# Gate pieces moved from the recurrence heads into prompt attention, and recurrence levels computed on half blocks

## The reference

```python
(q, k, v, iq, ik, iw, hq, hf, hi, hg, ga, gb) = jnp.split(h @ w_in, IN_OFFSETS, axis=-1)
...
merged = jax.nn.sigmoid(ga) * (attn @ w_proj_attn) + jax.nn.sigmoid(gb) * (o.reshape(B, T, WIDTH_B) @ w_proj_hgrn)
return merged @ w_out, k, v, ik, s_new
```

## Time and profile before

| | before |
|---|---|
| median of 3 runs (lowest to highest) | 1691.05 us (1688.89 to 1693.5) |
| time of the profiled execution | 1692.5 us |
| its span, first to last instruction | 1690.7 us |
| PE / DVE / ACT / POOL busy | 96% / 44% / 27% / 41% of the span |
| PE in the chain that ended last | 88% |
| mean granted TensorE clock | 0.983 |

### The profile page before, as it was taken

The page is one execution under the profiler, slowest core; times in us unless marked ns, Lnnn a source line. Parts: engine busy times, 40 slices in busy tenths (PEclk is TensorE's granted clock), DMA queues, the critical chain, the costliest instruction groups (busy, mean ns, idle before and its releaser), DMA issues.

```text
span 1690.7 us, 29123 instructions
## 1 busy us (share of the span) xinstructions
PE 1619.6 (96%) x12753; PEld 1498.2 (89%) x12753; DVE 735.9 (44%) x1138; ACT 452.3 (27%) x645; POOL 696.1 (41%) x580
## 2 busy tenths in 40 slices
PE   7999999999999999989889889988999999999998
PEld 6999999999976999988867655568999999999998
DVE  6422112224326689974587643345543321023221
ACT  4211112112354224422134333322232211112111
POOL 3443444546431345573542323334443343433432
PEclk9999999999999999997989899999999999999999
DMA  6322334333411232322252388995222322323222
GB/s 166 93 75 60 86 101 117 94 85 111 161 56 40 66 103 75 100 68 84 82 190 71 132 302 338 412 359 218 86 75 76 94 67 73 105 75 95 65 70 91
DMA packets 195230, 203.59 MB, mean 120 GB/s; under 512 B 6416, under 2 KB 181584, under 8 KB 186656
## 3 DMA queue, kind: packets, MB, share of 16 engines
q1 hardware_dynamic: 175344, 107.92, 22.3%
q0 software_dynamic: 12256, 77.93, 12.3%
q10 hardware_dynamic: 7504, 15.88, 2.5%
HBM read 187.21 MB, written 14.30 MB: 119 GB/s over the span
## 4 chain that ended last, share of the span: by engine, by line
PE 88%; DVE 7%; ACT 2%; issue 2%; DMA 1%; POOL 0%; SPq 0%; ACTq 0%; DVEq 0%
PE ps L1696 24%; PE ps L1697 24%; PE ps L1698 24%; PE ps L2167 4%; PE ps L2184 2%; PE ps L2242 1%; DVE att L1385 1%; DVE n_lo L1126 1%; DVE k_lev L1405 1%; PE ps L2075 1%; PE ps L2030 1%; PE ps L1709 1%; DVE prob_p L1467 1%; PE ps L2122 1%; DMA v_more<-in_cache_v,kv_row 1%
## 5 line engine op out<-in xcount | busy, mean ns | idle before, releaser
L528 POOL TENSOR_TENSOR w_lo<-raw,w_hi 128x512 fp32r<-128x512 f32 (+1 forms) x390 | 515.8, 1353 | 707.5 <-ACT w_hi L704 707.5
L1696 PE MATMUL ps<-n_lo,w_hi 128*128 128x288 f32 x1824 | 546.8, 300 | 1.0 <-ACT qT L818 1.0
L1697 PE MATMUL ps<-n_hi,w_lo 128*128 128x288 f32 x1824 | 540.1, 296 | 0.0
L1698 PE MATMUL ps<-n_hi,w_hi 128*128 128x288 f32 x1824 | 538.5, 295 | 0.0
L1696 PEld LDWEIGHTS ps<-n_lo,w_hi 128*128 128x128 f32 x1824 | 344.3, 189 | 11.2 <-issue 10.1
L1698 PEld LDWEIGHTS ps<-n_hi,w_hi 128*128 128x128 f32 x1824 | 345.5, 189 | 0.0
L1697 PEld LDWEIGHTS ps<-n_hi,w_lo 128*128 128x128 f32 x1824 | 344.7, 189 | 0.1
L704 ACT ACTIVATE w_hi<-raw 128x2048 fp32r<-128x2048 f32 (+2 forms) x108 | 188.2, 1742 | 273.3 <-PE ps L1698 271.1
L1697 PE MATMUL ps<-hid_hi,w_lo 128*128 128x288 f32 x704 | 208.4, 296 | 0.0
L1696 PE MATMUL ps<-hid_lo,w_hi 128*128 128x288 f32 x704 | 208.4, 296 | 0.0
L1698 PE MATMUL ps<-hid_hi,w_hi 128*128 128x288 f32 x704 | 208.1, 296 | 0.0
(11 more groups left out here) (305 smaller groups left out, 2246.6 us busy)
## 6 DMA issues: line engine op xcount, KB each, us to landing
raw<-in_ffn_w_gate SPq DMA_DIRECT2D x44, 512.0 KB, 4.0
raw<-in_ffn_w_up SPq DMA_DIRECT2D x44, 512.0 KB, 5.2
raw<-in_ffn_w_down SPq DMA_DIRECT2D x32, 704.0 KB, 4.6
raw<-in_w_in SPq DMA_DIRECT2D x22, 1024.0 KB, 5.3
gates<-scratch_g ACTq DMA_DIRECT2D x4, 1152.0 KB, 10.6
raw<-in_w_out SPq DMA_DIRECT2D x4, 1024.0 KB, 5.0
scratch_x<-xT ACTq DMA_DIRECT2D x1, 2304.0 KB, 12.1
scratch_g<-g_head SPq DMA_DIRECT2D x16, 144.0 KB, 1.8
```

The costliest lines, as they stand in the source:

```text
L528: ins = pool.tensor_tensor(w_lo[:, u % NRAW, part], raw[:, u % NRAW, part], w_hi[:, u % NW, part].bitcast(F32), ALU.subtract)
L1696: pe.matmul(dst, hi, x_lo, start=first, stop=False)
L1697: pe.matmul(dst, lo, x_hi, start=False, stop=False)
L1698: return pe.matmul(dst, hi, x_hi, start=False, stop=last)
```

## The change

1. `IN_HEADS` goes from 16 to 8: the pieces in the tails are gone. The heads keep the four of each pair's levels. Prompt attention has two pieces in each of steps 0 to 7 and one in each of steps 8 to 13. The second bank for pieces is bank 5, so in steps 0 to 7 both halves of a transpose go into bank 4 (`turn_banks`).
2. ACT copies a step's pieces out after the exponentials of the next step, not before. PE waits for a piece's bank through `gate_out`.
3. POOL's `low_part` inside the levels is gone; whole units are made low between them. Six units instead of four are scaled and stored by POOL in prompt attention, and one quarter instead of two is scaled at the projections.
4. Levels 1 to 7: the matmuls stream only the right halves, 64 columns a tile instead of 128, into 256 columns of a bank, and DVE's masked copy has 256 elements instead of 512. For the last two levels (b = 32 and 64) ACT copies the blocks without a mask (`block_out`).
5. `v_own` is made by DVE, between the levels and the state updates.
6. Five `EARLY` rounds instead of six. Four half rounds a step instead of three, so that the list ends in step 5; the exchange of lists is in step 7 and the work on the bias in steps 8 to 10.

```diff
-    return (3, 2, 0, 1)[n // 2]
+    return (n // 2 + 3) % 4
...
-        IN_HEADS = 16
-        UNITS_IN_HEADS = IN_HEADS // 4
-
+        IN_HEADS = 2 * HB
         STEPS = 2 * HA
-
-        def head_bank(i):
-
-            return i % 4 if i // 4 % 2 == 0 else (1, 6, 1, 0)[i % 4]
+        NARROW = HA
+
+        def pieces_of_step(m):
+
+            if m < NARROW:
+                return [IN_HEADS + 2 + 2 * m, IN_HEADS + 3 + 2 * m]
+            i = IN_HEADS + 2 + NARROW + m
+            return [i] if i < PIECES else []
+
+        def gate_bank(i):
+
+            if i < IN_HEADS:
+                return i % 4
+            if i == IN_HEADS:
+                return 6
+            return 5 if i % 2 == 0 and i < IN_HEADS + 2 + 2 * NARROW else 7
+
+        def score_banks(m):
+
+            return ps[:, 2 * (m % 2):2 * (m % 2) + 2, :]
+
+        def turn_banks(m):
+
+            return ps[:, 4, :].rearrange("p (e w) -> p e w", e=2) if m < NARROW else ps[:, 4:6, :]
...
+        def right_half(x, L):
+
+            return x.rearrange("p (n s b) -> p n s b", s=2, b=LEVELS[L])[:, :, 1, :]
+
+        ACT_LEVEL = 6
...
-                for n in range(UNITS_IN_HEADS, 8):
+                for n in range(2, 8):
...
-                for q in (2, 3):
-                    pool.wait_ge(S(f"quarter_in{q}"), X_IN[q] + 16)
-                    for n in range(2):
-                        for a in range(2):
-                            part = gates[:, GATES_AT[q] + n, a, :]
-                            ins = pool.tensor_tensor(part, part, rms[:, :], ALU.mult)
-                    ins.then_inc(S("gate_scaled"), 1)
+                pool.wait_ge(S("quarter_in3"), X_IN[3] + 16)
...
-                    if 3 <= L <= 6:
-                        low_part(L - 3)
...
-                lows(at_unit["gate", 2 * g + 2 if g == 0 else 4])
+                lows(at_unit["gate", g + 1])
                 state_store(2 * g)
                 state_store(2 * g + 1)
-            lows(at_unit["gate", 5])
+            lows(at_unit["gate", 3])
...
-            def own_values(h):
-
-                a, g = h % 2, h // 2
-                if g:
-                    act.wait_ge(S("head_read"), 2 * g)
-                else:
-                    act.wait_ge(S("prompt_biased"), 1)
-                for b in range(NB):
-                    ins = act.activation(v_own[:, a, b, :], stage[0:NS, g, 0, a * VD:(a + 1) * VD], ACT.Copy,
-                                         scale=cst[0:NS, C_OWN + NQ * b:C_OWN + NQ * b + 1])
-                ins.then_inc(S("v_own_done"), 1)
+            def block_out(g, a, L):
+
+                b = LEVELS[L]
+                act.wait_ge(S(f"level_done{a}"), 8 * g + L + 1)
+                act.wait_ge(S(f"level_out{a}"), 8 * g + L)
+                scores = ps[:, 4 + a, 0:256].rearrange("p (i n b) -> p i n b", i=4, b=b)
+                for n in range(P // (2 * b)):
+                    at = 2 * b * n
+                    ins = act.activation(att[at:at + b, a, :, at + b:at + 2 * b], scores[at:at + b, :, n, :], ACT.Copy)
+                ins.then_inc(S(f"level_out{a}"), 1)
 
             def heads(g):
-                act.wait_ge(S("stage_done"), NTOK + g + 1)
-                for a in range(2):
-                    own_values(2 * g + a)
-                for i in range(8 * g, 8 * g + 4):
+                for i in range(4 * g, 4 * g + 3):
                     gate_out(i)
+                for L in range(ACT_LEVEL, len(LEVELS)):
+                    for a in range(2):
+                        block_out(g, a, L)
+                gate_out(4 * g + 3)
...
-                    for i in range(8 * g + 4 + 2 * a, 8 * g + 6 + 2 * a):
-                        gate_out(i)
...
-                    if IN_HEADS + 1 + m < PIECES:
-                        if IN_HEADS + 1 + m == 28:
-                            act.wait_ge(S("pp_max"), m + 1)
-                        gate_out(IN_HEADS + 1 + m)
...
+                    for i in pieces_of_step(m - 1) if m else [IN_HEADS + 1]:
+                        gate_out(i)
                     if m:
                         turned(m - 1)
...
-            EARLY = 6
+            EARLY = 5
...
+                    b = LEVELS[L]
+                    n = P // (2 * b)
+                    if b < NQ:
+                        dve.copy_predicated(right_half(att_s[:, a, :], L), right_half(m[0:NS, 0:NS], L),
+                                            ps[0:NS, 6 + a, 0:NS // 2].rearrange("p (n b) -> p n b", b=b))
+                    dve.copy_predicated(mine.rearrange("p i (n s b) -> p i n s b", s=2, b=b)[:, :, :, 1, :],
+                                        right_half(m, L).unsqueeze(1).to_broadcast([P, 4, n, b]),
+                                        bank[:, 0:256].rearrange("p (i n b) -> p i n b", i=4, b=b)
+                                        ).then_inc(S(f"level_out{a}"), 1)
...
+                        if L - 1 < ACT_LEVEL:
+                            level_out(a, L - 1)
...
-                    level_out(a, 7)
+                for a in range(2):
+                    v0 = stage[0:NS, g, 0, a * VD:(a + 1) * VD]
+                    dve.tensor_tensor(v_own[:, a, :, :], v0.unsqueeze(1).to_broadcast([NS, NB, VD]),
+                                      cst[0:NS, C_OWN:C_OWN + NS:NQ].unsqueeze(2).to_broadcast([NS, NB, VD]),
+                                      ALU.mult).then_inc(S("v_own_done"), 1)
...
-                    for _ in range(3):
+                    for _ in range(4):
                         if taken[0] < 2 * ROUNDS:
                             take_half()
...
-                    if m == 7:
+                    if m == 5:
+                        assert taken[0] == 2 * ROUNDS
                         dve.engine_nop().then_inc(S("lists_done"), 1)
-                    if m == 9:
+                    if m == 8:
                         chosen_of_halves()
                         boundary()
+                    if m == 9:
+                        whole_rounds()
+                        last_round()
                     if m == 10:
-                        whole_rounds()
-                    if m == 11:
-                        last_round()
                         sample_biases()
...
-                if part[0] == 0 and not head:
-                    pe.wait_ge(S("gate_out"), i if i > IN_HEADS + 1 else i - 1)
-                bank = head_bank(i) if head else 6 if i == IN_HEADS else 7
+                if part[0] == 0 and i >= 4:
+                    one = i >= IN_HEADS + 2 + 2 * NARROW
+                    pe.wait_ge(S("gate_out"), i - 3 if i < IN_HEADS else i if one else i - 1)
+                bank = gate_bank(i)
...
+                            for t in range(1, NT):
+                                ins = pe.matmul(ps[:, 4 + a, P * (t - 1):P * t], key[:, h, cols(t)], query[:, h, cols(t)],
+                                                start=True, stop=True)
+                        else:
+                            if LEVELS[L] < NQ:
+                                pe.matmul(ps[0:NS, 6 + a, 0:NS // 2], k_lev[:, a, 0:NS], right_half(q_lev[:, a, 0:NS], L),
+                                          start=True, stop=True)
+                            for t in range(1, NT):
+                                ins = pe.matmul(ps[:, 4 + a, 64 * (t - 1):64 * t], k_lev[:, a, cols(t)],
+                                                right_half(q_lev[:, a, cols(t)], L), start=True, stop=True)
                         ins.then_inc(S(f"level_done{a}"), 1)
-                    gate_piece(8 * g + L // 2, (L % 2,))
+                    gate_piece(4 * g + L // 2, (L % 2,))
...
-                    if a:
-                        pe.wait_ge(S("o_out"), 2 * g + 1)
-                    else:
-                        pe.wait_ge(S("gate_out"), 8 * g + 4)
-                    tail = 8 * g + 4 + 2 * a
-                    gate_piece(tail, (0,))
-                    pe.wait_ge(S("k_rows_done"), 2 * g + 2)
+                    pe.wait_ge(S("k_rows_done"), h + 1)
+                    pe.wait_ge(S("gate_out"), 4 * g + 4)
...
-                            gate_piece(*((tail, (1,)), (tail + 1, (0,)), (tail + 1, (1,)))[i - 1])
...
+                    if m == NARROW:
+                        pe.wait_ge(S("gate_out"), IN_HEADS + 1 + 2 * NARROW)
...
+                dots(0)
                 pe.wait_ge(S("state_s_done"), HB)
-                dots(0)
                 gate_piece(IN_HEADS + 1, (0, 1))
...
-                    if IN_HEADS + 2 + m < PIECES:
-                        gate_piece(IN_HEADS + 2 + m, (0, 1))
+                    for i in pieces_of_step(m):
+                        gate_piece(i, (0, 1))
                     if m:
                         values(m - 1)
                     turn(m)
```

More of the change, by code:

```diff
@@ L510, in _ @@
                 load_unit(u)
[L511 removed]
+                if n in (0, 1):
                     store_piece(4 * n + 3)
@@ L529, in lows @@
                                                  w_hi[:, u % NW, part].bitcast(F32), ALU.subtract)
```

(10 more changed lines are left out.)

78 lines of the change are left out of this document (38 added, 40 removed).

## The result

The changed kernel takes 1701.4 us (median; 1700.26 to 1703.58) against 1691.05 for the kernel before: a ratio of 1.0063, 95% interval 1.0047 to 1.0079. Slower by 0.6%, outside the range, on the side to which the forecast gave 0.18. What follows splits up the 7.9.

A forecast was written before the change was run, and what follows sets the result against it. PE, busy 96% of the span, was taken to bound the kernel. Levels -6.2, tails -21.5 and prompt attention +22 sum to -5.7 us: from 1692.5, less 1.45 to the median, 1685.4, put at 1686; range 1675 to 1699.

The forecast's parts named there:

- Levels, -6.2: Levels of both head pairs: 3.1 us less a pair, 6.2 in all, from 3 to 9.
- (2): Levels: POOL's w_lo part of 1.48 us leaves four levels of each pair, which helps DVE too.
- (1): Levels: DVE's att copy shrinks to 128x256, about 0.27 us less, twice a level; ACT copies in the last two.
- (3): Levels: matmuls stream 64 columns instead of 128, at 0.24 us each instead of 0.27, saving 0.3 us a level.
- Tails, -21.5: Tails of both head pairs: eight half pieces fewer in each, 21.5 us less together, from 9 to 29.
- one tail of each kind: Tails: one at full clock, one with low clock after its first head; 14.5 + 7 = 21.5 us gained.
- rival (C): Tails: clock low from the first state update on; +7 to +10 us, 1698 with both tails; chance 0.22.
- Prompt attention, +22: Prompt attention with eight more pieces: 20.4 us more in steps 0 to 7, 1.7 in 8 to 13; 18 to 27.
- the wait for piece A: Prompt attention, steps 0 to 7: PE waits 0.7 us a step for ACT's later bank copy, 5.2 us in all.
- the half-clock prices: Tails at low clock: second head's updates 5.3 us for 2.5, sample matmuls 3.4 for 2.2, v_own matmuls 3.5 for 1.9.
- A's 0.16: Rival on the tails: both keep the full clock, gain 29 us instead of 21.5, so 1678; chance 0.16.
- The argument against (C): Tails: the clock outlived 1.95 us of near idleness ahead of 836.84, longer than the 1.5 us wait in question.

The follow-up runs named there:

- e5: The kernel of e2 with POOL's subtraction of the next gate unit held until both k transposes are done; ratio to the kernel before 0.9995.
- e1: The changed kernel with POOL's low part of a gate unit back in four quarters in levels 3 to 6; ratio to the kernel before 1.0007.
- e2: The changed kernel with v_own made by ACT at the start of the heads, as before the change; ratio to the kernel before 1.0015.
- e10: The changed kernel with v_own on ACT, POOL's unit after the k transposes and ACT's piece copies ahead of the exponentials; ratio to the kernel before 0.9921.
- e14: The kernel of e10 with v_own left on DVE, as in the changed kernel; ratio to the kernel before 0.9945.
- e8: The changed kernel with ACT's piece copies ahead of a step's exponentials in prompt attention, as before the change; ratio to the kernel before 1.0000.
- e15: The changed kernel with seven of the eight eight-column matmuls of each head left out; ratio to the kernel before 1.0025.
- e9: The changed kernel itself measured once more, nothing changed; ratio to the kernel before 1.0057.

## Why the prediction was wrong, step by step

- **Levels, -6.2: measured -5.2.** The period of 3.5 us came where it was said (from level 4 to level 7 of pair 0: 3.4, 3.5, 3.6). Level 2 of pair 0 took 6.6 us where pair 1's took 4.4, 1.7 us of it for the clock at half. The reason was in part wrong: of the three edits put together there, (2), POOL's quarters, carries 3.5 to 4.0 us, and (1) and (3) together 1.2 to 1.7, which the clock in pair 0 takes back. Term (3), 0.3 us a level, measured 0.2 in level 4. The sentence from the Trainium skill on cost by columns (TensorE: Matmul & The Clock Gate, Back-to-back issue gap) was rightly set aside: half the columns took 1.89 us where all took 2.08.
- **Tails, -21.5: measured -12.5. This is the step that failed.** Two terms in it, the second much the larger. First, DVE's last four products were not priced beside POOL's whole unit, though the prediction named that neighbour for v_own: they took 6.6 us instead of the 3.3 of e5, so the first state update came 8.1 us after the last level's first matmul and not 6.7, and the state copy at 10.7 and not 8.7. That made tail 0 1.4 us longer at full clock than the 22.7 laid out (24.1 without the clock's part), and tail 1 no longer (22.0, as laid out). Second, the clock: "one tail of each kind" supposed one tail at full clock and priced the two at 7.5 us (29 - 21.5); both were near 0.75, and the clock's part was 15.3. That is rival (C) in its price, +7 to +10, which is what was measured. In its mechanism it fits tail 1, where the clock was at half from the state updates on; in tail 0 it fell only at the first head's end. That the two moves together bring this loss is shown by e1 and e2; both have the 110 us of heads (138.5 - 6.2 - 21.5 = 110.8) that the prediction gave to the changed kernel. That the waits act through the clock is not shown: e10 and e14 lost 9.2 and 11.0 us to it without them.
- **Prompt attention, +22: measured +25.2.** Steps 0 to 7 were right in their number, 20.4 against 19.6, and the wait for piece A at 0.7 us is there (4.7 us in all, said 5.2). As a price that term was too high: with the waits removed in e8 only 1.0 us came back in these steps. Steps 8 to 13 were put at 1.7 and took 3.9: the waits for the bank cost 3.1, as said (3.3), but DVE's wait of 1.6, which was to go, became one of 2.2. Steps 14 and 15 were not costed and took 1.7.
- **The sum.** -5.7 became +7.5: 9.0 from the tails, 3.2 from prompt attention, 1.0 from the levels. Two slips in the working change little: the half-clock prices add up to 7.2 us a tail, which leaves 9 and 6 and not 8 and 6, and two thirds of 0.36 with A's 0.16 give 0.40 for faster, not 0.43.
- **The argument against (C)**, that the clock outlived the sample matmuls ahead of 836.84, rested on one tail with dense pieces around them. No row of before shows a tail without pieces, so nothing there supported one such tail at full clock; the runs since have tails of the same code at different clocks (tail 0 of after and of e8 at 0.74 and 0.83).

## What to carry to other kernels

Work moved off one engine's queue must be priced on its new one beside what the neighbours run at that moment: here a GpSimd unit and a VectorE job, harmless one at a time, together held the first state up and cost 11 us, most of it through the granted clock. When dense matmuls are taken out of a serial stretch, price what is left at a lower clock too unless a trace shows otherwise: here such tails were granted anything from 0.65 to 1.00. Then look at where the moved work stands in each engine's queue: three such places (own values, POOL's unit, the copies of the pieces) turned +0.6% into -0.8%.

## What the runs showed that was not expected

- In the two tails, 3.1 and 5.9 us less waiting went with 11.8 and 15.9 us less time (e2, e1); most of the difference is the granted clock. It fell in tails whose longest wait was 2.75 us, didn't fall in two that had the same wait (e2 and e15, tail 1), and fell in tails with no wait above 1.54 us (e10).
- Three executions with the same code in the tails took 61.4, 61.3 and 58.1 us in them (after, e9, e8), and 46.1, 46.1 and 46.4 when the clock's part is taken out: the scatter was the clock alone.
- Levels of half width lost 1.7 us to the clock in pair 0 in all fourteen kernels that have them; levels of full width lost nothing there in any of three.
- Eight matmuls with 128x128 weights took 1.89 us at 64 columns, 2.08 at 128 and 1.95 at 8: half the columns are not half the time.
- DVE and POOL slow each other: 0.74 us to 1.83 for a product of 576 columns, 4.94 us to 7.04 for POOL's unit.
